# Where the low halves of the next head's q and k are computed in a stick-breaking attention: GpSimd or VectorE

## The chip, the cores and the metric

One NeuronCore of a Trainium2 chip runs the whole program. The metric is the device time of one execution in microseconds (us). The engines are TensorE (PE; its weight loads are shown as PEld), VectorE (DVE), ScalarE (ACT), GpSimd (POOL) and SyncE (SP), which here only issues DMAs.

## The reference

Two transformer blocks over 1024 positions of width 1024, in float32: a first block (dilated attention, latent attention, a mixture of experts), then a second one of two layers. The change lies in the first layer of the second block, in its stick-breaking attention, 8 heads of 64 dimensions. Cut to what matters:

```python
z = einsum('bthd,bshd->bhts', q[:, q0:kend], k[:, :kend]) * d ** -0.5
strict = s_idx < t_idx
log_beta = log_sigmoid(z)
log_one_minus = where(strict, log_sigmoid(-z), 0.0)
suffix = cumsum(log_one_minus, axis=3, reverse=True) - log_one_minus
w = where(strict, exp(log_beta + suffix), 0.0)
out = einsum('bhts,bshd->bthd', w, v[:, :kend])
```

The kernel computes the same as a product: sigmoid(z) times the running product of sigmoid(-z) over the keys to the right.

## The kernel before

`stick_breaking` is one stage of the program, between the retention and the output mix. It has the chip to itself: stages are separated by barriers. Its work is 64 tiles T: 8 heads of 8 tiles i = 0 to 7, where tile i holds 128 queries and n = (i+1)*128 keys. Every engine runs its own instruction list, written as a function `body(l, T)` that `tiles` unrolls 16 tiles at a time (the first 8 tiles and the last stretch stand apart, three rounds of a loop of 16 between); l is T modulo 16. The engines meet only by semaphores.

What each engine does in its step T, in this order:

- PE (lines 2664 to 2705): the scores of tile T into PSUM buffer `sb_s` (two buffers, so it waits until the scan of tile T-2 has ended); then the transposes of w(T-3) into `sb_t` (one buffer: waits until wT(T-4) is copied out); then the product of wT(T-4) with v into `sb_op`.
- ACT (lines 2717 to 2736): two sigmoids of the scores, sigmoid(z) to `be` and sigmoid(-z) in place; then for wide tiles its part of the copy of wT(T-3); at i = 3 the rounding of the next head's q and k (`split_hi`, lines 2713 and 2714).
- DVE (lines 2756 to 2776): its part of the copy of wT(T-3) (line 2763); the scan of tile T, a running product (line 2768), which reads the scores' PSUM buffer and `ones`; the copy of the result of tile T-4 (`sb_ob`, line 2776). The scan waits until w(T-2) has been computed.
- POOL (lines 2781 to 2799): w(T) = be * pr (line 2787), two operands in SBUF.

The scores are computed from q and k each split in a rounded part (type fp32r in the rows) and the rest. ACT rounds the whole (`qs`, `kh`), and somebody must subtract: `qs[64:128]` = q minus its rounded value (64 partitions by 1024), `kl` = k minus its rounded value (128 by 1024). Each of the two counts 4 on `lo_ok`. The buffers are double, one for each of two heads (u = 0, 1), and the split for head h+1 is made while head h runs. PE waits for both at its head's first tile, and SP waits for them before it loads the raw q and k of the head after next. The first head's split is made on DVE ahead of the loop (`split_lo`, lines 2746 and 2747). Those of the other seven heads are made on POOL: the q part behind w of tile i = 3 (line 2793), the k part behind w of tile i = 4 (line 2798), each with a wait for the w before it and one for its own end.

Of the kernel before, what the change touches and what calls it, by code (L numbers as in the profile page):

```python
# [7 lines left out]
F32 = mybir.dt.float32  # L8
F32R = mybir.dt.float32r
U32 = mybir.dt.uint32  # L10
ALU = mybir.AluOpType
# [3 lines left out]
P = 128  # L15
# [903 lines left out]
def tiles(eng, total, peel, lag, body):  # L919


    for T in range(peel):
        body(T % TURN, T)
    with eng.Fori(0, total // TURN - 1) as r:
        for l in range(peel, peel + TURN):
            body(l % TURN, r * TURN + l)
    for T in range(total - TURN + peel, total + lag):
        body(T % TURN, T)


def active(T, k, total):

    return not isinstance(T, int) or 0 <= T - k < total


def reached(eng, sem, n):

    if not isinstance(n, int) or n > 0:
        eng.wait_ge(sem, n)
# [1643 lines left out]
def stick_breaking(nc, ident, heads, qkT_in, v_in_d, C, out):  # L2583
# [4 lines left out]
    T8, DV = NT, 64  # L2588
    total = heads * T8
    widths = [(i + 1) * P for i in range(T8)]  # L2590
    with stage(nc) as st:
        qraw, kraw = (st.sb("sb_" + n, [P, 2, S]) for n in ("qraw", "kraw"))
        qs, kh, kl = (st.sb("sb_" + n, [P, 2, S], F32R) for n in ("qs", "kh", "kl"))
# [23 lines left out]
        def halves(i):  # L2617

            return min(i + 1, BANK // P), i + 1

        with nc.Block() as block:
# [120 lines left out]
            @block.vector  # L2742
            def _(dve):
                def split_lo(u, n_hi):
                    dve.wait_ge(hi_ok, n_hi)
                    dve.tensor_tensor(qs[64:P, u, :], qraw[64:P, u, :], qs[64:P, u, :].bitcast(F32), ALU.subtract).then_inc(lo_ok, 4)
                    dve.tensor_tensor(kl[:, u, :], kraw[:, u, :], kh[:, u, :].bitcast(F32), ALU.subtract).then_inc(lo_ok, 4)

                dve.memset(ones[:, :], 1.0).then_inc(ones_ok, 1)
                dve.memset(pr[:, :, S:S + 1], 1.0).then_inc(ones_ok, 1)  # L2750
                dve.tensor_copy(eye[:, :], ident[:, :]).then_inc(far_ok, 1)
                dve.wait_ge(consts_in, 16)
                dve.tensor_scalar(far[:, :], masks[:, 1, :], NEG, None, ALU.mult).then_inc(far_ok, 1)
                split_lo(0, 8)
                dve.wait_ge(ones_ok, 2)

                def body(l, T):
                    if active(T, 3, total):
                        m = (l - 3) % TURN
                        a, _ = halves(m % T8)  # L2760
                        reached(dve, turned_a, T - 2)
                        reached(dve, pv_done, T - 4)
                        dve.tensor_copy(wT[:, m % 2, 0:a * P], tps[:, 0:a * P]).then_inc(wT_a, 1)
                    if active(T, 0, total):
                        n = widths[l % T8]
                        dve.wait_ge(om_ok, T + 1)
                        reached(dve, w_ok, T - 1)
                        dve.tensor_tensor_scan(pr[:, l % 2, S - n:S][:, ::-1], sps[l % 2][:, 0:n][:, ::-1], ones[:, 0:n], 1.0,  # L2768
                                               ALU.mult, ALU.mult).then_inc(pr_ok, 1)
                    if active(T, 4, total):  # L2770
                        m = (l - 4) % TURN
                        u, i = m // T8, m % T8
                        reached(dve, pv_done, T - 3)
                        if i == 0:
                            dve.wait_ge(stored[u], T - 4 - 8 * u + 16)
                        dve.tensor_copy(o[:, u, i, :], ops[m % 2][:, 0:DV]).then_inc(o_done, 1)
                tiles(dve, total, 8, 4, body)

            @block.gpsimd
            def _(pool):  # L2780
                def body(l, T):
                    if active(T, 0, total):
                        n = widths[l % T8]
                        pool.wait_ge(be_ok, T + 1)
                        pool.wait_ge(pr_ok, T + 1)
                        reached(pool, turned_b, T - 3)
                        pool.tensor_tensor(w[:, l % 4, 0:n], be[:, l % 4, 0:n], pr[:, l % 2, S - n + 1:S + 1],  # L2787
                                           ALU.mult).then_inc(w_ok, 1)
                        u = 1 - l // T8
                        if l % T8 == 3 and active(T + 5, 0, total):  # L2790
                            pool.wait_ge(hi_ok, T + 5 + 4)
                            pool.wait_ge(w_ok, T + 1)
                            pool.tensor_tensor(qs[64:P, u, :], qraw[64:P, u, :], qs[64:P, u, :].bitcast(F32), ALU.subtract).then_inc(lo_ok, 4)
                            pool.wait_ge(lo_ok, T + 9)
                        if l % T8 == 4 and active(T + 4, 0, total):
                            pool.wait_ge(hi_ok, T + 4 + 8)
                            pool.wait_ge(w_ok, T + 1)
                            pool.tensor_tensor(kl[:, u, :], kraw[:, u, :], kh[:, u, :].bitcast(F32), ALU.subtract).then_inc(lo_ok, 4)
                            pool.wait_ge(lo_ok, T + 12)
                tiles(pool, total, 8, 0, body)  # L2800


# [637 lines left out]
```

## Time and profile before

| what | us |
|---|---|
| median of 3 runs | 2599.95 |
| lowest and highest | 2592.92 and 2613.81 |
| the profiled execution, its own time | 2613.81 |
| its span in the profile | 2612.0 |
| first scan of the stage starts, at | 1717.06 |
| last w of the stage starts, at | 1885.75 |

The profiled execution is one of the three. All places in time below are us from the start of its span. A row of the timeline has the start, the length, the engine, the line, the operation, what it writes and reads, and how often; in brackets the idle time of the engine before it and what ended it. Tiles are told apart by their width: the scan of 128x640 is tile i = 4, 128x768 is i = 5, 128x896 is i = 6, 128x1024 is i = 7.

### The profile page before, as it was taken

The page shows a single profiled execution, that of the slowest core. Times are in us where ns is not written, and L with a number is a line of the kernel's source. Part 1 is how long each engine was busy: PE and PEld are TensorE (multiplying, and loading weights), DVE is VectorE, ACT ScalarE, POOL GpSimd, SP SyncE. Part 2 cuts the span into 40 slices and gives each one's busy share as a digit, 9 for nine tenths or more (in the row PEclk, how much of TensorE's full clock was granted, in tenths as well). Part 3 has the DMA queues.
Part 4 walks back from the last instruction along what each step waited for, and adds up shares of the span by engine and source line. Part 5 has one row for each costly group of instructions (what it writes and reads, how often), then busy time and mean ns, then how long its engine had stood idle before and what let it go on. Part 6 is the DMA issues. An engine that isn't in the chain of part 4 may idle for free. (4 is left out here: it accounts for less than half of the span.)

```text
span 2612.0 us, 34392 instructions
## 1 busy us (share of the span) xinstructions
PE 2218.1 (85%) x12244; PEld 1825.9 (70%) x12244; DVE 1290.0 (49%) x2211; ACT 1029.8 (39%) x1828; POOL 584.1 (22%) x672
## 2 busy tenths in 40 slices
PE   7996997999797599999289997968859799956768
PEld 5885887999685466675278885758748687845657
DVE  3333665555543666665451210357755343417843
ACT  3333654555431255554231210046543233327632
POOL 1003101522010122231110001446522000027822
PEclk9997998999898699999699998579989899987879
DMA  4787776321344399995652312243163424141152
GB/s 152 215 239 198 221 219 165 98 64 40 118 146 171 126 359 370 355 342 209 217 206 97 113 49 77 61 87 73 37 219 108 153 95 148 69 135 47 42 184 90
DMA packets 216721, 399.15 MB, mean 153 GB/s; under 512 B 90513, under 2 KB 111377, under 8 KB 203905
## 3 DMA queue, kind: packets, MB, share of 16 engines
q1 hardware_dynamic: 177008, 314.52, 38.0%
q10 hardware_dynamic: 28384, 61.62, 6.2%
q0 software_dynamic: 11184, 21.13, 2.2%
q8 instruction: 87, 1.43, 0.2%
q14 instruction: 58, 0.47, 0.1%
HBM read 300.16 MB, written 114.85 MB: 159 GB/s over the span
## 5 line engine op out<-in xcount | busy, mean ns | idle before, releaser
L78 PE MATMUL pe_acc<-pe_w,hT 128*128 128x512 f32 x960 | 222.3, 393 | 0.0
L78 PEld LDWEIGHTS pe_acc<-pe_w,hT 128*128 128x128 f32 x960 | 181.7, 190 | 37.8
L78 PE MATMUL ex_gu<-hT,ex_xT 128*128 128x512 f32 x792 | 194.2, 401 | 0.8 <-DVE hT L2349 0.8
L2349 DVE TENSOR_TENSOR hT<-ex_raw,hT 128x2048 fp32r<-128x2048 f32 x66 | 150.9, 2288 | 87.1 <-ACT hT L2320 87.1
L78 PE MATMUL pg_acc<-hT,pg_w 128*128 128x512 f32 x768 | 180.0, 396 | 8.9 <-DVE pg_w L257 8.9
L78 PEld LDWEIGHTS pg_acc<-hT,pg_w 128*128 128x128 f32 x768 | 145.5, 190 | 42.4 <-DVE pg_w L257 9.3
L78 PEld LDWEIGHTS ex_gu<-hT,ex_xT 128*128 128x128 f32 x792 | 147.4, 189 | 34.5 <-DVE hT L2349 1.2
L2320 ACT ACTIVATE hT<-ex_raw 128x2048 fp32r<-128x2048 f32 x66 | 126.2, 1913 | 41.4 <-PEq L47 23.9
L296 DVE COPY pe_o<-pe_acc 128x512 f32<-128x512 f32 x28 | 19.3, 690 | 206.7 <-PE pe_acc L78 206.7
L1725 PE MATMUL ab_op<-ab_v,ab_pT 128*128 128x64 f32 x1024 | 121.3, 272 | 0.0
L2278 PE MATMUL ex_dn<-ex_wd,ex_hT 128*128 128x512 f32 x264 | 118.7, 592 | 0.8 <-ACT ex_hT L2314 0.8
L1725 PEld LDWEIGHTS ab_op<-ab_v,ab_pT 128*128 128x128 f32 x1024 | 119.3, 192 | 0.0
L1736 DVE TENSOR_REDUCE ab_mx<-ab_s 128x1 f32<-128x1024 f32 x64 | 78.4, 1224 | 72.3 <-PE ab_s L1703 72.3
L849 PE MATMUL om_acc<-om_w,hT 128*128 128x512 f32 x384 | 95.5, 408 | 18.0 <-DVE om_w L825 16.6
L78 PE MATMUL pa_acc<-hT,pa_w 128*128 128x512 f32 (+1 forms) x432 | 100.1, 392 | 0.7 <-DVE pa_o L290 0.6
L849 PEld LDWEIGHTS om_acc<-om_w,hT 128*128 128x128 f32 x384 | 74.1, 196 | 36.2 <-DVE om_w L825 19.4
L2787 POOL TENSOR_TENSOR sb_w<-sb_be,sb_pr 128x128 f32<-128x128 f32 (+3 forms) x64 | 76.6, 1205 | 97.3 <-DVE sb_pr L2768 75.4
L2768 DVE TENSOR_TENSOR_SCAN sb_pr<-sb_s,sb_ones 128x128 f32<-128x128 f32 (+3 forms) x64 | 86.7, 1354 | 20.0 <-ACT sb_s L2725 17.6
L849 PE MATMUL am_acc<-am_w,hT 128*128 128x512 f32 x384 | 91.6, 398 | 3.4 <-DVE hT L690 3.4
L1515 ACT ACTIVATE aa_p<-aa_sc,aa_nm 128x256 f32<-128x256 f32 x128 | 63.9, 500 | 75.6 <-DVE aa_nm L1482 74.1
L78 PEld LDWEIGHTS pa_acc<-hT,pa_w 128*128 128x128 f32 (+1 forms) x432 | 77.9, 182 | 22.5 <-DVE pa_o L290 3.2
L849 PE MATMUL em_acc<-em_w,hT 128*128 128x512 f32 x384 | 91.2, 397 | 2.6 <-DVE hT L690 2.6
(473 smaller groups left out, 4990.9 us busy)
## 6 DMA issues: line engine op xcount, KB each, us to landing
ex_raw<-in_w_gate SPq DMA_DIRECT2D x33, 1024.0 KB, 7.2
ex_raw<-in_w_up SPq DMA_DIRECT2D x33, 1024.0 KB, 11.1
ex_wd<-in_w_down SPq DMA_DIRECT2D x33, 1024.0 KB, 14.2
pe_raw<-in_even_w_in SPq DMA_DIRECT2D x6, 2048.0 KB, 9.1
pg_raw<-in_odd_w_in SPq DMA_DIRECT2D x5, 2048.0 KB, 9.4
scr_q<-pa_o SPq DMA_DIRECT2D x32, 256.0 KB, 3.8
scr_k<-pa_o SPq DMA_DIRECT2D x32, 256.0 KB, 3.8
hT<-scr_k SPq DMA_DIRECT2D x16, 512.0 KB, 6.8
```

The costliest lines, as they stand in the source:

```text
L78: mm = pe.matmul(out, a(p, k), b(q, k), start=(k == 0 and i == 0), stop=(k == n - 1 and i == 2))
L296: dve.tensor_copy(obuf[0:m, u, 0:n], acc[u][0:m, 0:n]).then_inc(copied[u], 1)
L849: mm = pe.matmul(acc[t % 2][:, nn], hT[:, p, k, t * P:(t + 1) * P], w[:, q, k, nn], start=(i == 0 and j == 0), stop=(i == 7 and j == 2))
L1515: act.activation(p[:, T % 4, a, :], sc[:, T % 2, a, :], ACT.Exp, bias=nm[:, T % 4, a:a + 1], scale=0.125, accum_out=ml[:, a, i, 1, h:h + 1 ...
L1725: mm = pe.matmul(ops[m % 2][:, 0:DV], pT[:, m % 2, k * P:(k + 1) * P], v[:, u, k, :], start=(k == 0), stop=(k == NT - 1))
L1736: dve.reduce_max(mx[:, l:l + 1], sps[l % 2][:, :], AX.X).then_inc(max_done, 1)
L2278: mm = pe.matmul(dn[:, n * BANK:(n + 1) * BANK], hTs[:, b % 2, k, :], wd[:, b % ND, k * D + n * BANK:k * D + (n + 1) * BANK], start=(k == ...
L2320: act.activation(split(s, HI)[:, :, g, :], raw[:, s % NW, g, :].rearrange("p (k n) -> p k n", k=8), ACT.Copy).then_inc(w_hi, 1)
L2349: dve.tensor_tensor(split(s, LO)[:, :, g, :], raw[:, s % NW, g, :].rearrange("p (k n) -> p k n", k=8), split(s, HI)[:, :, g, :].bitcast(F3 ...
L2768: dve.tensor_tensor_scan(pr[:, l % 2, S - n:S][:, ::-1], sps[l % 2][:, 0:n][:, ::-1], ones[:, 0:n], 1.0, ALU.mult, ALU.mult).then_inc(pr_o ...
L2787: pool.tensor_tensor(w[:, l % 4, 0:n], be[:, l % 4, 0:n], pr[:, l % 2, S - n + 1:S + 1], ALU.mult).then_inc(w_ok, 1)
```

## The change

The two subtractions for the next head are taken from POOL and given to DVE, both at i = 4, between the scan of tile 4 and the copy of the result of tile 0, by the function that already does it for the first head. POOL's waits on its own results go too.

```diff
@@ block.vector, body @@
                         dve.tensor_tensor_scan(pr[:, l % 2, S - n:S][:, ::-1], sps[l % 2][:, 0:n][:, ::-1], ones[:, 0:n], 1.0,
                                                ALU.mult, ALU.mult).then_inc(pr_ok, 1)
+                        if l % T8 == 4 and active(T + 4, 0, total):
+                            split_lo(1 - l // T8, T + 4 + 8)
@@ block.gpsimd, body @@
                         pool.tensor_tensor(w[:, l % 4, 0:n], be[:, l % 4, 0:n], pr[:, l % 2, S - n + 1:S + 1],
                                            ALU.mult).then_inc(w_ok, 1)
-                        u = 1 - l // T8
-                        if l % T8 == 3 and active(T + 5, 0, total):
-                            pool.wait_ge(hi_ok, T + 5 + 4)
-                            pool.wait_ge(w_ok, T + 1)
-                            pool.tensor_tensor(qs[64:P, u, :], qraw[64:P, u, :], qs[64:P, u, :].bitcast(F32), ALU.subtract).then_inc(lo_ok, 4)
-                            pool.wait_ge(lo_ok, T + 9)
-                        if l % T8 == 4 and active(T + 4, 0, total):
-                            pool.wait_ge(hi_ok, T + 4 + 8)
-                            pool.wait_ge(w_ok, T + 1)
-                            pool.tensor_tensor(kl[:, u, :], kraw[:, u, :], kh[:, u, :].bitcast(F32), ALU.subtract).then_inc(lo_ok, 4)
-                            pool.wait_ge(lo_ok, T + 12)
```

DVE's list inside the loop, around tile 4 of a head, before (the scan is named SCALAR_TENSOR_TENSOR here; `sb_pr` is its result, `sb_wT` the transposed weights, `sb_ob` the output):

```order
L2763 COPY sb_wT<-sb_t 128x256
L2766 REGISTER_ALU
L2768 SCALAR_TENSOR_TENSOR sb_pr<-sb_s,sb_ones 128x640
L2775 REGISTER_ALU
L2776 COPY sb_ob<-sb_op 128x64
L2763 COPY sb_wT<-sb_t 128x384
L2766 REGISTER_ALU
L2768 SCALAR_TENSOR_TENSOR sb_pr<-sb_s,sb_ones 128x768
```

The same place of DVE's list in the changed kernel:

```order
L2763 COPY sb_wT<-sb_t 128x256
L2766 REGISTER_ALU
L2768 SCALAR_TENSOR_TENSOR sb_pr<-sb_s,sb_ones 128x640
L2745 REGISTER_ALU
L2746 TENSOR_TENSOR sb_qs<-sb_qraw,sb_qs 64x1024
L2747 TENSOR_TENSOR sb_kl<-sb_kraw,sb_kh 128x1024
L2777 REGISTER_ALU
L2778 COPY sb_ob<-sb_op 128x64
L2763 COPY sb_wT<-sb_t 128x384
L2766 REGISTER_ALU
L2768 SCALAR_TENSOR_TENSOR sb_pr<-sb_s,sb_ones 128x768
```

The two subtractions stand ahead of the copy of tile 0's result, of the wT copy of tile 2 (128x384) and of the scan of tile 5.

POOL's list inside the loop, tiles 3 to 6, before:

```order
L2787 TENSOR_TENSOR sb_w<-sb_be,sb_pr 128x512
L2791 REGISTER_ALU
L2793 TENSOR_TENSOR sb_qs<-sb_qraw,sb_qs 64x1024
L2784 REGISTER_ALU
L2787 TENSOR_TENSOR sb_w<-sb_be,sb_pr 128x640
L2796 REGISTER_ALU
L2798 TENSOR_TENSOR sb_kl<-sb_kraw,sb_kh 128x1024
L2784 REGISTER_ALU
L2787 TENSOR_TENSOR sb_w<-sb_be,sb_pr 128x768
```

And in the changed kernel:

```order
L2789 TENSOR_TENSOR sb_w<-sb_be,sb_pr 128x512
L2786 REGISTER_ALU
L2789 TENSOR_TENSOR sb_w<-sb_be,sb_pr 128x640
L2786 REGISTER_ALU
L2789 TENSOR_TENSOR sb_w<-sb_be,sb_pr 128x768
```

POOL has only the w of each tile left. The lists of PE, ACT and SP are the same in both kernels.

## Rows read from the trace of the kernel before

**Rows 1.** Stretches: length, busy PE, PEld, DVE, ACT, POOL (x count), clock, DMA, GB/s.

```profile
1745.00:1766.00 21.00, 18.77 (x140) 16.94 (x140) 16.06 (x25) 13.52 (x23) 14.30 (x10) 1.00 0.35 76
...
257.80:261.20 3.40, 3.40 (x19) 3.40 (x18) 1.72 (x8) 1.67 (x6) 1.40 (x4) 0.50 1.06 382
...
2396.00:2404.80 8.80, 3.26 (x67) 2.79 (x62) 5.97 (x14) 8.71 (x15) 4.29 (x6) 1.00 0.97 241
```

**Rows 2.** Groups of instructions of POOL: a subtraction that moves.

```profile
L2798 POOL TENSOR_TENSOR sb_kl<-sb_kraw,sb_kh 128x1024 fp32r<-128x1024 f32 x7 | 16.6, 2375 | 1.2 <-POOL sb_w L2787 1.2
```

**Rows 3.** Timeline of DVE: scan 4 of the second head, third head's tiles 4 to 7.

```profile
1749.31 1.49 DVE L2768 TENSOR_TENSOR_SCAN sb_pr<-sb_s,sb_ones 128x640 f32<-128x640 f32 x1 [0.79 <-ACT sb_s L2725]
...
1770.44 1.49 DVE L2768 TENSOR_TENSOR_SCAN sb_pr<-sb_s,sb_ones 128x640 f32<-128x640 f32 x1 [0.79 <-ACT sb_s L2725]
...
1771.96 0.55 DVE L2763 COPY sb_wT<-sb_t 128x384 f32<-128x384 f32 x1
1772.78 1.76 DVE L2768 TENSOR_TENSOR_SCAN sb_pr<-sb_s,sb_ones 128x768 f32<-128x768 f32 x1 [0.27 <-ACT sb_s L2725]
...
1775.21 2.02 DVE L2768 TENSOR_TENSOR_SCAN sb_pr<-sb_s,sb_ones 128x896 f32<-128x896 f32 x1
...
1777.26 0.68 DVE L2763 COPY sb_wT<-sb_t 128x512 f32<-128x512 f32 x1
1778.05 2.29 DVE L2768 TENSOR_TENSOR_SCAN sb_pr<-sb_s,sb_ones 128x1024 f32<-128x1024 f32 x1
```

**Rows 4.** Timeline of POOL, the same head: w of tile 4, then of tiles 5 and 6.

```profile
1772.27 1.32 POOL L2787 TENSOR_TENSOR sb_w<-sb_be,sb_pr 128x640 f32<-128x640 f32 x1 [0.25 <-POOL sb_qs L2793]
...
1776.38 3.28 POOL L2787 TENSOR_TENSOR sb_w<-sb_be,sb_pr 128x768 f32<-128x768 f32 x2 [0.24 <-POOL sb_kl L2798]
```

**Rows 5.** Timeline of PE, the same head: end of scores 6, scores 7, transposes 5.

```profile
1773.06 0.23 PE L2676 MATMUL sb_s<-sb_far,sb_eye 128*128 128x128 f32 x1
...
1774.68 0.47 PE L2673 MATMUL sb_s<-sb_kh,sb_qs 128*128 128x512 f32 x1
...
1778.35 0.84 PE L2685 MATMUL sb_t<-ident,sb_w 128*128 128x128 f32 x6 [0.51 <-ACT sb_wT L2732]
```

**Rows 6.** Timeline of ACT, the same head: second sigmoid of tile 7.

```profile
1777.01 1.01 ACT L2725 ACTIVATE sb_s<-sb_s 128x1024 f32<-128x1024 f32 x1
```

**Rows 7.** Timeline of DVE, ahead of the stage's loop: the first head's two subtractions.

```profile
1712.84 1.22 DVE L2746 TENSOR_TENSOR sb_qs<-sb_qraw,sb_qs 64x1024 fp32r<-64x1024 f32 x1 [1.55 <-ACT sb_kh L2714]
1714.10 1.23 DVE L2747 TENSOR_TENSOR sb_kl<-sb_kraw,sb_kh 128x1024 fp32r<-128x1024 f32 x1
```

**Rows 8.** Timeline of POOL and DVE in the retention stage.

```profile
1629.00 1.86 POOL L2470 TENSOR_TENSOR re_t<-re_x,re_cs 128x256 f32<-128x256 f32 x2
1629.03 1.24 DVE L2532 TENSOR_TENSOR re_dec<-re_rot,re_rowdec 128x512 f32<-128x512 f32 x1 [11.49 <-POOL re_rot L2473]
...
1637.14 0.72 POOL L2472 TENSOR_TENSOR re_rot<-re_t 128x256 f32<-128x256 f32 x1
...
1638.58 0.69 DVE L2532 TENSOR_TENSOR re_dec<-re_rot,re_rowdec 128x512 f32<-128x512 f32 x1 [2.22 <-POOL re_rot L2473]
```

**Rows 9.** Timeline of DVE and POOL behind the mixture of experts.

```profile
1323.87 1.28 DVE L614 SCALAR_TENSOR_TENSOR e_y<-e_e,gates,e_x 128x1024 f32<-128x1024 f32 x1 [1.76 <-issue]
1324.02 1.54 POOL L546 TENSOR_TENSOR e_rs<-e_ms,e_half 128x1 f32<-128x1 f32 x1
1325.19 1.28 DVE L617 SCALAR_TENSOR_TENSOR e_y<-e_e,gates,e_y 128x1024 f32<-128x1024 f32 x1
```

**Rows 10.** Timeline of DVE and PE, the first head: scan 4, transposes 3.

```profile
1724.41 1.49 DVE L2768 TENSOR_TENSOR_SCAN sb_pr<-sb_s,sb_ones 128x640 f32<-128x640 f32 x1 [1.02 <-ACT sb_s L2725]
...
1728.93 1.05 PE L2685 MATMUL sb_t<-ident,sb_w 128*128 128x128 f32 x4
```

**Rows 11.** Timeline of PE in two other stages: gaps ahead of a matmul.

```profile
256.38 0.66 PE L1450 MATMUL aa_op<-aa_vn,aa_pT 128*128 128x64 f32 x4 [1.85 <-DVE aa_pT L1489]
...
2398.66 0.33 PE L3129 MATMUL hg_x<-hg_qk 128*64 128x64 f32 x2 [1.84 <-ACT hg_cross L2986]
```

## The prediction

> **What bounds the kernel now.** I read the busy shares by stretch first. In a steady head of the stick-breaking stage (21 us; scan 4 comes again after 1770.44 - 1749.31 = 21.13 [rows 3]) PE is busy 18.77 us, DVE 16.06, POOL 14.30, and the TensorE clock is granted in full [rows 1]. By shares DVE has 5 us a head to spare, and the change moves about 2.5 us of DVE work in. Shares say nothing of where the idle time lies, so the second view is DVE's timeline over one head [rows 3]: at tile i of a head DVE does wT(i-3), scan(i), ob(i-4). From the scan of i=4 (640 columns, starts 1770.44) to that of i=7 (1024 columns, starts 1778.05) it is all but full. Scan 5 starts 1772.78, where the wT copy before it ends 1772.51 and the next would start 0.04 earlier (1772.47): slack 0.31. Scan 6 starts 1775.21, 0.67 after scan 5 ends, which two copies (ob and wT, 0.2 and 0.68 less their overlaps) fill: no slack. Scan 7 starts 1778.05 where DVE was ready at 1777.26 + 0.68 - 0.04 = 1777.90: slack 0.15; that small wait is for POOL, whose w of tile 5 (the first, some 1.5 us, of the pair at 1776.38) ends about 1777.9 [rows 4]. DVE's idle time lies in tiles 0 to 3, where PE has many transposes and products and sets the pace.
>
> So a head is a chain: PE's order from the end of scan 7 to the scores of tile 4, then ACT, then DVE from scan 4 to scan 7. The new work goes into the last link.
>
> **What is removed.** Seven times two POOL subtractions of 2.37 us, 33.2 us in all (16.6 for each line; one of the two stands in [rows 2]). What waits on POOL there is w(4) at 1772.27, 0.34 after scan 4's end (1771.93), and w(5), which costs scan 7 its 0.15. Nothing else is late behind them. The self-waits go with them. SP's loads for head h+2 wait for the same count, are issued some 2 us earlier or at about the same time, and land a head before they are needed: nothing.
>
> **What is added.** The same two subtractions on DVE behind scan 4, 1.22 and 1.23 us [rows 7], with a start lag of 0.04 before each (their rows at 1712.84 and 1714.10 leave 0.04 between them; other DVE neighbours overlap by 0.08). ACT's halves, which they wait for, are done before scan 4 starts. Bare price: 0.04+1.22+0.04+1.23 = 2.53 us behind scan 4. Queued behind it on DVE are ob(0), wT(2) and scan 5; PE's transposes of tile 3 wait for wT(2), PE's scores of tile 7 for scan 5.
>
> The bare price is the lower bound, since scan 4 also releases w(4) on POOL, and the subtractions and w both read two SBUF operands. The nearest rows are of the retention stage [rows 8]: a DVE instruction of that kind takes 0.69 alone, but 1.24 when it starts 0.03 behind a POOL one (1629.00), and the two POOL ones there take 1.86 together where their like take 0.72 each. One stands still while the other runs. In the MoE epilogue a POOL instruction begins behind a DVE one (1323.87 to 1325.15), ends 1325.56, and the next DVE one starts 1325.19 [rows 9]: POOL came in at the gap of 0.04. I apply both: first subtraction 1771.97 to 1773.19, w(4) waits and then runs 1.18 (its 1.32 less the 0.14 start that is behind it), to 1774.37; the second, held meanwhile, runs on for 1.13, to 1775.50. Price 3.57 us. If POOL is not let in at the gap it is 2.53. I take 3.57, because the gap of 0.04 stands in both rows 7 and rows 9.
>
> The page "SBUF — State Buffer" of the Trainium skill, section "SBUF: two separate sides", says that a DVE instruction with two SBUF inputs and a GpSimd instruction that reads SBUF exclude each other for the whole instruction, whoever is first. By that rule the sum is the one with 3.57, without it 2.53; rows 8 agree.
>
> **A steady head.** DVE's path: 3.57 - 0.31 - 0.15 = 3.11 later at scan 7. ACT's path: scan 5 ends 1772.47+3.57+1.76 = 1777.80; PE's scores of tile 7 start 0.06 later. From their start before (1774.68 [rows 5]) to the second sigmoid's end (1778.02 [rows 6]) it is 3.34, and 0.03 more to a scan: 1781.23, which is 3.2 later than 1778.05. So scan 7 is 3.2 us late. Next on PE are the transposes of tile 5 at 1778.35, released by ACT's wT copy behind that sigmoid, then the scores of tile 1 and the transposes of tile 6, released by scan 7 and the DVE copy behind it: all shift alike, and in PE's stretch nothing gives the time back. Six heads (the 2nd to the 7th; the last has no split): 19.2 us. With 2.53 the same working gives 2.17 a head, 13.0.
>
> **The first head** runs at half clock and has room: scan 4 ends 1724.41 + 1.49 = 1725.90, PE's transposes of tile 3 start only at 1728.93 [rows 10]. Subtractions to 1729.47; the wT(2) copy (0.55) to 1730.05, so the transposes start some 1.2 late, and the rest with them: +1.2 (with 2.53: 0.1).
>
> **The clock.** PE now stands between the end of scores 6 (1773.29 [rows 5]) and the end of wT(2): 1775.50 + 0.55 + 0.1 = 1776.15, a gap of 2.86 us where there is none today. After a gap of 1.85 before 256.38 [rows 11] the granted clock fell to 0.5 from 257.8 to 261.2 [rows 1]; after one of 1.84 before 2398.66 it stayed [rows 11, 1]. A low stretch of 3.4 us costs at most half its length, 1.7, and nothing where PE isn't what is waited for. Bounds 0 and 6 x 1.7 = 10.2; I take 4 us in all (a fall in four heads, 1 us each).
>
> **Sum.** 19.2 + 1.2 + 4 = 24 us. The stage has no work beside it and ends in a barrier, so the next stage starts that much later. The profiled execution took 2613.81 (span 2612.0): 2638 by it. It was the slowest of the three; against their median of 2599.95 it is 2624.
>
> **Rivals.**
> A: POOL isn't let in at the gap, or DVE isn't held by it. For it: in its favour only that no row shows a long POOL instruction slipping between two DVE ones; the row at 1325 is a short one. 13.0+0.1, and 1 or 2 for the clock (the gap is 1.8 us): 2614.
> B: POOL was the engine to relieve, and DVE's idle 5 us takes the work in. For it: the shares of rows 1, the wait of scan 7 for w(5). It gives the small waits back, 0.34 x 7 = 2.4: 2597.5, and would be decided if DVE's free time lay behind scan 4. Against: rows 3.
> C, clearly slower: the clock falls in every head, and for two low stretches, since PE after the gap waits again for wT and scan 5 at low duty. Place: from tile 7 into the next head's tiles 0 and 1, which PE sets. 20.4 + 6 x 3.4 = 41, 2641. It decides when low stretches reach past scan 7. Against: within the first head the clock rose while PE had waits too.
>
> **How the numbers follow.** Forecast 0.47, A 0.28, C 0.15, B 0.06, the rest something unseen. About 1% is what a measurement of this kernel can tell from no change; that is 26 us, and the forecast's 24 is just inside it. Its own range, 2612 to 2636, goes over 1% in some 45 of 100; C does throughout, A hardly: slower 0.38. Faster by 1% has no mechanism, 0.03. Same 0.59. The range holds A and the half of C: 2604 to 2643.
>
> **What would show it.** Right: DVE's two subtractions behind each 640-column scan; the second 2.3 us long, not 1.23; w(4) about 2.3 to 2.4 instead of 1.32; the period from one scan 4 to the next 24.2 us or a bit over instead of 21.1; PE's transposes of tile 3 with some 2.8 us of idle before them, released by DVE's wT; low clock of a few us in the stage after 1740. Wrong: a second subtraction of 1.23 (then A), a period of 21 (then B), other stages changed in length.

## The result, and the profile after

The changed kernel takes 2628.48 us (median of 4 runs, 2624.34 to 2632.24) against 2596.43 us for the kernel before (median of 4): the ratio is 1.0115, 95% interval 1.0084 to 1.0147, 30 us by the ratio and 32 by the medians. The forecast was 24 us slower.

The profiled execution of the changed kernel has a span of 2623.3 us, only 11.3 above that of the kernel before. Two stages moved, in opposite ways. The first group of rows is the busy time in stretches (length, then busy us and instruction count of PE, PEld, DVE, ACT and POOL, granted clock, DMA share, GB/s) of the kernel before: the retention stage, then the stick-breaking stage.

```profile
1617.00:1700.00 83.00, 68.45 (x304) 49.70 (x304) 24.25 (x57) 5.14 (x16) 34.77 (x48) 0.55 0.26 80
1717.00:1888.00 171.00, 151.20 (x1065) 135.84 (x1066) 128.24 (x188) 105.83 (x170) 109.77 (x78) 0.94 0.26 58
```

The same two stages in the changed kernel, and then three pieces of the second: from the scan of tile 4 of one head to that of the next, for the second, third and fourth head.

```profile
1622.00:1681.00 59.00, 44.80 (x304) 32.86 (x304) 24.48 (x57) 5.25 (x16) 34.92 (x48) 0.83 0.36 112
1697.50:1900.10 202.60, 167.87 (x1070) 150.86 (x1070) 152.03 (x202) 106.75 (x171) 83.67 (x64) 0.85 0.22 48
1730.98:1759.80 28.82, 24.24 (x141) 22.57 (x140) 19.59 (x26) 13.75 (x22) 10.57 (x8) 0.76 0.25 55
1759.80:1786.01 26.21, 21.40 (x143) 19.13 (x142) 19.57 (x27) 13.75 (x22) 10.58 (x8) 0.87 0.27 61
1786.01:1812.01 26.00, 21.35 (x141) 19.39 (x140) 19.61 (x27) 13.75 (x22) 10.58 (x8) 0.87 0.28 61
```

Stick-breaking went from 170.7 us (first scan to end of the last w) to 202.6, which is 31.9 more, and fits. The retention stage, which the change doesn't touch, took 83 us in the profiled execution before and 59 in the one after: it ran at a granted clock of 0.55 in one and 0.83 in the other. The same unchanged stage took 58 to 64 us in seven of the nine profiled executions here and 83 in two (see the end), so I take this as chance and not as the change. It is why the two spans must not simply be subtracted. A head took 21.09 us on the mean before (scan 4 to scan 4, 2nd to 7th head) and takes 26.21 now.

Inside a head, DVE's timeline of the changed kernel, to be held against [rows 3]:

```profile
1730.98 1.49 DVE L2768 TENSOR_TENSOR_SCAN sb_pr<-sb_s,sb_ones 128x640 f32<-128x640 f32 x1 [0.79 <-ACT sb_s L2725]
...
1759.80 1.49 DVE L2768 TENSOR_TENSOR_SCAN sb_pr<-sb_s,sb_ones 128x640 f32<-128x640 f32 x1 [0.79 <-ACT sb_s L2725]
1761.33 1.22 DVE L2746 TENSOR_TENSOR sb_qs<-sb_qraw,sb_qs 64x1024 fp32r<-64x1024 f32 x1
1762.58 2.23 DVE L2747 TENSOR_TENSOR sb_kl<-sb_kraw,sb_kh 128x1024 fp32r<-128x1024 f32 x1
...
1764.86 0.54 DVE L2763 COPY sb_wT<-sb_t 128x384 f32<-128x384 f32 x1
1765.33 1.74 DVE L2768 TENSOR_TENSOR_SCAN sb_pr<-sb_s,sb_ones 128x768 f32<-128x768 f32 x1
...
1767.70 2.01 DVE L2768 TENSOR_TENSOR_SCAN sb_pr<-sb_s,sb_ones 128x896 f32<-128x896 f32 x1
...
1771.31 0.69 DVE L2763 COPY sb_wT<-sb_t 128x512 f32<-128x512 f32 x1 [1.48 <-PE sb_t L2685]
1772.55 2.29 DVE L2768 TENSOR_TENSOR_SCAN sb_pr<-sb_s,sb_ones 128x1024 f32<-128x1024 f32 x1 [0.55 <-ACT sb_s L2725]
```

The k subtraction takes 2.23 us, where the same instruction takes 1.23 in [rows 7]. From scan 4 to scan 5 it is now 5.53 us; before it was 2.34. And scan 7 no longer follows at once behind scan 6: DVE waits 1.48 us for PE's transposes and 0.55 us for ACT. POOL in the same head:

```profile
1761.43 2.30 POOL L2789 TENSOR_TENSOR sb_w<-sb_be,sb_pr 128x640 f32<-128x640 f32 x1 [2.58 <-DVE sb_pr L2768]
1767.20 1.54 POOL L2789 TENSOR_TENSOR sb_w<-sb_be,sb_pr 128x768 f32<-128x768 f32 x1 [3.48 <-DVE sb_pr L2768]
```

w(4) takes 2.30 us, where [rows 4] has 1.32: it starts 0.10 behind the start of the q subtraction, which ends at 1762.55, and itself ends at 1763.73, 1.18 later; the k subtraction ends at 1764.81, 1.08 after w(4). So each of the two looks as if it had stood while the other ran. PE in the same head, to be held against [rows 5], and ACT's second sigmoid of tile 7 [rows 6]:

```profile
1762.41 0.22 PE L2676 MATMUL sb_s<-sb_far,sb_eye 128*128 128x128 f32 x1
1765.51 1.09 PE L2685 MATMUL sb_t<-ident,sb_w 128*128 128x128 f32 x4 [2.88 <-issue]
1766.98 1.51 PE L2703 MATMUL sb_op<-sb_v,sb_wT 128*128 128x64 f32 x6 [0.39 <-ACTq L2734]
1768.25 0.77 PE L2673 MATMUL sb_s<-sb_kh,sb_qs 128*128 128x512 f32 x1
...
1770.11 0.31 PE L2676 MATMUL sb_s<-sb_far,sb_eye 128*128 128x128 f32 x1
...
1772.85 0.85 PE L2685 MATMUL sb_t<-ident,sb_w 128*128 128x128 f32 x6 [0.17 <-ACT sb_wT L2732]
```

```profile
1771.51 1.01 ACT L2725 ACTIVATE sb_s<-sb_s 128x1024 f32<-128x1024 f32 x1
```

PE stands idle for 2.88 us before the transposes of tile 3, which wait for DVE's copy of wT(2), 1764.86 to 1765.40; in the other five heads from the 2nd to the 7th the gap is 3.02. Behind the gap everything on PE is slow. The clock says why (a stretch of the head before, then two of this one):

```profile
1737.30:1750.90 13.60, 13.30 (x61) 12.94 (x60) 9.24 (x13) 4.38 (x9) 5.93 (x5) 0.50 0.01 1
...
1764.60:1771.40 6.80, 5.50 (x22) 4.78 (x22) 5.32 (x9) 0.95 (x1) 3.10 (x2) 0.50 0.18 39
1771.40:1791.90 20.50, 15.94 (x123) 14.47 (x122) 15.34 (x22) 12.81 (x22) 7.49 (x7) 1.00 0.34 72
```

For 6.8 us from 1764.6 the granted clock is 0.50 (1.2 GHz), then 1.00 again (2.4 GHz); in the head before it stayed low for at least the 13.6 us shown. The scores of tile 7 start at 1768.25, where with scan 5 ending at 1767.07 they could have started at 1767.13, because the four transposes take 1.09 us and the product behind them 1.51, and the scores stand behind both in PE's list.

### The profile page after: what moved, and what is told of

Read it like the earlier page. It is cut to its first block and busy times, and to the rows that moved or that the text cites. A ratio compares the mean times of both kernels' runs of the same rounds, so it can differ in the third digit from the quotient of the medians.

```text
span 2623.3 us, 34380 instructions
## 1 busy us (share of the span) xinstructions
PE 2214.6 (84%) x12244; PEld 1828.5 (70%) x12244; DVE 1314.7 (50%) x2225; ACT 1030.5 (39%) x1828; POOL 554.7 (21%) x658
## 3 DMA queue, kind: packets, MB, share of 16 engines
q8 instruction: 87, 1.43, 0.2%
## 5 line engine op out<-in xcount | busy, mean ns | idle before, releaser
L2789 POOL TENSOR_TENSOR sb_w<-sb_be,sb_pr 128x128 f32<-128x128 f32 (+3 forms) x64 | 83.7, 1312 | 148.1 <-DVE sb_pr L2768 139.7
## 6 DMA issues: line engine op xcount, KB each, us to landing
ex_wd<-in_w_down SPq DMA_DIRECT2D x33, 1024.0 KB, 13.6
```

## The experiments

Periods below are from scan 4 of a head to scan 4 of the next, mean over the 2nd to the 7th head; stage lengths are from the first scan to the end of the last w. All come from the profiled execution of the run. Ratios are against runs of the kernel before on the same chip. Compare runs by the period: the first head's own period lies between 23.00 and 26.15 us over the nine profiles, in part because the low clock with which the stage begins ended 13.4 to 14.0 us after the first scan in three of them and 18.5 to 20.5 us after it in the other six, and the stage length carries this too.

**Matmuls against the gap.** Edit, on PE ahead of the scores:

```diff
                         reached(pe, pr_ok, T - 1)
+                        if i == 6 and not (isinstance(T, int) and T < 8):
+                            for _ in range(10):
+                                pe.matmul(sps[l % 2][:, 0:BANK], qs[:, u, i * P:(i + 1) * P], kh[:, u, 0:BANK], start=True, stop=True)
```

> The changed kernel plus ten matmuls of 128x512 whose result is overwritten, put on PE just ahead of the scores of tile 6 in heads 2 to 8, where PE has nothing to do for 2.9 us a little later. They hold the scores of tile 6 back by 2.2 us, to about 1.5 us before DVE is ready for their scan. Theory (two terms: a longer DVE chain and a low clock after the gap): granted clock 1.00 through heads 2 to 7, period from scan 4 to scan 4 down from 26.2 to 24.2 or 24.3 us, second subtraction still 2.23 us, stage from first scan to last w 191 us instead of 202.6, so about 2617 us. Rival (the clock is a bystander and the chain through DVE and the queues is simply longer than I worked out): period stays at 26 or rises, also at full clock.

Measured: 2610.77 us (10 runs), ratio 1.0063 (1.0035 to 1.0090). Period 24.18, stage 192.7. Stretches of the stage and of one head, then PE and DVE in the next head:

```profile
1699.80:1892.50 192.70, 168.70 (x1133) 149.12 (x1134) 151.11 (x202) 105.77 (x170) 83.77 (x64) 0.94 0.23 51
1733.30:1757.50 24.20, 21.20 (x152) 18.80 (x151) 19.51 (x27) 13.65 (x22) 10.60 (x8) 1.00 0.30 67
```

```profile
1759.01 2.56 PE L2672 MATMUL sb_s<-sb_kh,sb_qs 128*128 128x512 f32 x10
...
1763.17 0.63 PE L2688 MATMUL sb_t<-ident,sb_w 128*128 128x128 f32 x4 [0.74 <-issue]
...
1760.24 2.23 DVE L2750 TENSOR_TENSOR sb_kl<-sb_kraw,sb_kh 128x1024 fp32r<-128x1024 f32 x1
```

More work on PE made the stage 9.9 us shorter than in the changed kernel (the two ratios, 1.0063 and 1.0115, have intervals that just touch). The gap is 0.74 us, the clock stays at 1.00 through the head, the k subtraction is as long as before the edit. So the clock is a term of its own, 26.21 - 24.18 = 2.03 us a head, and not a companion of the longer chain. Its rival (the period stays) falls. Taken head by head (period less 24.18), the changed kernel pays 4.6 us where the low stretch was 13.7 us long, 1.8 to 2.0 where it was 6.8 (three heads), 0.9 to 1.0 where it was 3.4 (two heads).

**w(4) behind both subtractions.** Edit, on POOL:

```diff
                         reached(pool, turned_b, T - 3)
+                        if l % T8 == 4 and active(T + 4, 0, total):
+                            pool.wait_ge(lo_ok, T + 12)
                         pool.tensor_tensor(w[:, l % 4, 0:n], be[:, l % 4, 0:n], pr[:, l % 2, S - n + 1:S + 1],
```

> The changed kernel with one wait more: POOL starts w of tile 4 only when both subtractions on DVE have ended. Theory (DVE and POOL shut each other out, and w(4) comes in between the two subtractions): second subtraction 1.23 instead of 2.23 us, w(4) 1.32 instead of 2.30, DVE's price 2.5 us, PE's gap 1.8 instead of 2.9 us; period 23.3 us where the clock stays up and up to 25 where it falls after the smaller gap; stage 182 to 193 us. Rival (w(4) is needed early and the added wait makes it worse, or the 2.23 us have another cause such as the buffer's own waits): period 26.2 or more, second subtraction still above 2 us.

Measured: 2617.71 us (10 runs), ratio 1.0087 (1.0054 to 1.0121). Stage 187.8. DVE, POOL and PE in one head:

```profile
1770.16 1.22 DVE L2746 TENSOR_TENSOR sb_qs<-sb_qraw,sb_qs 64x1024 fp32r<-64x1024 f32 x1
1771.41 1.23 DVE L2747 TENSOR_TENSOR sb_kl<-sb_kraw,sb_kh 128x1024 fp32r<-128x1024 f32 x1
```

```profile
1772.72 1.33 POOL L2791 TENSOR_TENSOR sb_w<-sb_be,sb_pr 128x640 f32<-128x640 f32 x1 [5.03 <-DVE sb_kl L2747]
...
1773.34 0.63 PE L2685 MATMUL sb_t<-ident,sb_w 128*128 128x128 f32 x4 [2.02 <-issue]
```

A wait that was added, and with it the lock between the two engines is gone: k 1.23, w(4) 1.33, and nobody is late for w(4). The gap is still 2.0 us (1.8 was expected), and the clock still falls, in five of the six heads: periods 23.82, 23.76, 23.68, 25.15 and 23.89, and 23.16 in the one head without a low stretch. By the whole time this run can't be told from the changed kernel (1.0087 against 1.0115, intervals that overlap; its retention stage took 83 us); the shorter stage is what shows the gain.

**Both.** The changed kernel with the two edits above together.

> Both at once: POOL's w(4) behind the subtractions, and the ten matmuls ahead of the scores of tile 6. Theory: nothing is left but the bare price of DVE, 2.53 less the slack of 0.46 and 0.1 for ACT's way: period 23.3 us, granted clock 1.00 after the first head, stage about 184 us. Rival (there is a third term): period clearly above 23.3.

Measured: period 23.21, in every head between 23.18 and 23.24; stage 184.5. One execution took 2610.33 us. The stage:

```profile
1704.30:1888.80 184.50, 164.81 (x1139) 146.34 (x1140) 144.50 (x202) 106.04 (x171) 76.83 (x64) 0.96 0.24 53
```

Nothing is left beside the bare length of DVE's work. With the wait alone, the one head without a low stretch had 23.16 and no extra matmul in it, which agrees: what the matmuls win is the clock. The three terms of a head are now apart: 23.21 - 21.09 = 2.12 bare, 24.18 - 23.21 = 0.97 for the lock, 26.21 - 24.18 = 2.03 for the clock; together 5.12.

**No gap between the two subtractions.** Edit: `qs[64:P, u, :]` and `qraw[64:P, u, :]` of the q subtraction become `qs[:, u, :]` and `qraw[:, u, :]`; the high part of q is lost with it in half of the partitions.

> The changed kernel with the q subtraction on all 128 partitions instead of 64 to 127 (it spoils the high part of q in partitions 0 to 63, so the scores lose it; the count and the length of the instructions stay). Both subtractions then begin on the same partition. Theory (POOL gets in because DVE leaves 0.04 us between two instructions that begin on different partitions): the two follow each other with an overlap of 0.08 us, w(4) waits for both and takes 3.5 us or more, the second subtraction takes 1.23 us; period as in the run with the wait. Rival (POOL comes in between two DVE instructions whether there is a gap or not): second subtraction 2.2 us, w(4) 2.3 us, period 26.

Measured: period 26.1, stage 201.8, 2616.68 us in one execution. DVE, then POOL, in one head:

```profile
1756.45 1.20 DVE L2746 TENSOR_TENSOR sb_qs<-sb_qraw,sb_qs 128x1024 fp32r<-128x1024 f32 x1
1757.56 2.34 DVE L2747 TENSOR_TENSOR sb_kl<-sb_kraw,sb_kh 128x1024 fp32r<-128x1024 f32 x1
```

```profile
1756.66 2.16 POOL L2789 TENSOR_TENSOR sb_w<-sb_be,sb_pr 128x640 f32<-128x640 f32 x1 [2.58 <-DVE sb_pr L2768]
```

The second instruction now begins 0.09 us before the first ends, so the gap is gone, and still w(4) comes in between: it ends at 1758.82 and k takes 2.34. My theory of the gap falls, its rival holds: POOL, waiting, gets its turn between two DVE instructions with or without a pause.

**Only q moves.** The k subtraction stays on POOL, DVE has

```diff
+                        if l % T8 == 4 and active(T + 4, 0, total):
+                            u = 1 - l // T8
+                            dve.wait_ge(hi_ok, T + 4 + 8)
+                            dve.tensor_tensor(qs[64:P, u, :], qraw[64:P, u, :], qs[64:P, u, :].bitcast(F32), ALU.subtract).then_inc(lo_ok, 4)
```

> Half the change: only the q subtraction goes to DVE behind scan 4, the k subtraction stays on POOL behind w(4). Theory (a head pays what DVE's chain from scan 4 to scan 7 is lengthened by, less its slack of 0.46, and the clock only where PE's gap grows long): price 0.04 + 1.22, so 0.8 us a head, PE's gap ahead of the transposes of tile 3 about 0.7 us and the clock at 1.00: period 21.9 us instead of 21.1, stage some 5 us longer than before. w(4) is held back by the q subtraction to about 2.3 us, and POOL's k subtraction starts later, so w(5) ends near 1779.3 in the times of rows 3 and 4, which is 1.2 us later than scan 7 starts: if that wait counts, the period is 22.4. Rival (work on DVE costs its full length, 2.2 us or more a head as soon as it stands behind scan 4): 23 or more.

Measured: period 22.16 in each of the six heads, within 0.02; stage 175.7; 2597.60 us in one execution. The stage, then DVE, POOL and ACT in one head:

```profile
1697.20:1872.90 175.70, 151.00 (x1064) 133.90 (x1065) 136.76 (x195) 105.71 (x170) 99.99 (x71) 0.96 0.26 56
```

```profile
1751.72 1.22 DVE L2773 TENSOR_TENSOR sb_qs<-sb_qraw,sb_qs 64x1024 fp32r<-64x1024 f32 x1
1752.97 0.22 DVE L2780 COPY sb_ob<-sb_op 128x64 f32<-128x64 f32 x1
...
1758.13 0.68 DVE L2763 COPY sb_wT<-sb_t 128x512 f32<-128x512 f32 x1
1758.91 2.29 DVE L2768 TENSOR_TENSOR_SCAN sb_pr<-sb_s,sb_ones 128x1024 f32<-128x1024 f32 x1
```

```profile
1756.90 3.28 POOL L2791 TENSOR_TENSOR sb_w<-sb_be,sb_pr 128x768 f32<-128x768 f32 x2 [0.24 <-POOL sb_kl L2797]
```

```profile
1757.87 1.01 ACT L2725 ACTIVATE sb_s<-sb_s 128x1024 f32<-128x1024 f32 x1
```

1.07 a head, between the two values that I gave (0.8 and 1.3), and by neither's working: w(5) ends near 1758.4, and scan 7 starts at 1758.91, 0.03 behind the end of ACT's sigmoid, so w(5) isn't waited for. From scan 4 to scan 5 it is now 3.49 us, against 2.17 on the mean of the same six heads before (2.34 in the head of [rows 3], which had more slack at scan 5 than the others): 1.32 more, of which the copy behind the subtraction is 0.11, since it starts 0.03 after its end where it otherwise starts 0.08 before the end of what precedes it. From scan 5 to scan 7 it is 0.25 less than before, where five of the six heads had waited for w(5). The rival's price of 2.2 us or more is far off. Half of the change costs a fifth of the whole: PE's gap is 0.9 us and the clock stays at 1.00, and the lock holds only w(4), since no second subtraction stands on DVE.

**The same work on DVE, two tiles earlier.** ACT's rounding goes from tile 3 to tile 1, and on DVE, in place of the call behind scan 4:

```diff
+                        if l % T8 in (2, 3) and active(T + 8 - l % T8, 0, total):
+                            u = 1 - l // T8
+                            dve.wait_ge(hi_ok, T + 16 - l % T8)
+                            if l % T8 == 2:
+                                dve.tensor_tensor(qs[64:P, u, :], qraw[64:P, u, :], qs[64:P, u, :].bitcast(F32), ALU.subtract).then_inc(lo_ok, 4)
+                            else:
+                                dve.tensor_tensor(kl[:, u, :], kraw[:, u, :], kh[:, u, :].bitcast(F32), ALU.subtract).then_inc(lo_ok, 4)
```

> The same work on the same engine as in the changed kernel, at another place: ACT rounds the next head's q and k at tile 1 instead of 3, DVE subtracts q behind scan 2 and k behind scan 3, where it waits for PE today. Theory (place, not engine or amount, makes the cost): no lengthening, the small waits for POOL at scan 7 go as well: period 20.8 to 21.1 us, clock 1.00, stage 168 to 171 us against 170.7, total equal to before within 0.1 per cent or 2 us better. Rival (2.5 us of DVE work more a head, and the lock against w, cost time wherever they stand): period 22 to 24.

Measured: 2593.93 us (12 runs) against 2591.88 (23 runs) of the kernel before, ratio 1.0007 (0.9985 to 1.0029): no difference. Period 20.91, stage 169.1. The stage, then DVE and POOL:

```profile
1701.60:1870.70 169.10, 148.70 (x1064) 133.37 (x1065) 143.50 (x202) 104.81 (x170) 89.06 (x64) 0.95 0.27 58
```

```profile
1752.01 1.20 DVE L2776 TENSOR_TENSOR sb_kl<-sb_kraw,sb_kh 128x1024 fp32r<-128x1024 f32 x1
...
1754.23 1.49 DVE L2768 TENSOR_TENSOR_SCAN sb_pr<-sb_s,sb_ones 128x640 f32<-128x640 f32 x1 [0.56 <-ACT sb_s L2725]
```

```profile
1752.22 1.93 POOL L2794 TENSOR_TENSOR sb_w<-sb_be,sb_pr 128x512 f32<-128x512 f32 x1 [1.12 <-DVE sb_pr L2768]
```

Same engine and same amount, and it costs nothing, since scan 4 waits for ACT anyway. The lock is there too, but it holds only POOL (w(3) takes 1.93 instead of 1.09, k 1.20): the two subtractions no longer follow each other, so none of them stands behind a w. The place, which includes their standing apart, made the 32 us, and neither the engine nor the amount.

**Earlier on POOL.** The kernel before with ACT's rounding at tile 1 and POOL's subtractions behind w(2) and w(3):

```diff
-                        if l % T8 == 3 and active(T + 5, 0, total):
-                            pool.wait_ge(hi_ok, T + 5 + 4)
+                        if l % T8 == 2 and active(T + 6, 0, total):
+                            pool.wait_ge(hi_ok, T + 6 + 8)
...
-                        if l % T8 == 4 and active(T + 4, 0, total):
-                            pool.wait_ge(hi_ok, T + 4 + 8)
+                        if l % T8 == 3 and active(T + 5, 0, total):
+                            pool.wait_ge(hi_ok, T + 5 + 8)
```

> The kernel before with the same earlier places: ACT rounds at tile 1, POOL subtracts q behind w(2) and k behind w(3), where it idles 2 us or more a tile; DVE has none of it. Theory: only the small waits behind POOL go (w(4) and w(5) in time): period 20.7 to 20.9 instead of 21.1, stage 168 to 169 us, 2 us in 2600, at the edge of what can be measured. Rival (POOL was worth relieving for more than that): stage below 166 us. Second rival (PE's transposes now wait for w(2) or w(3), which the subtractions hold back): period above 21.3.

Measured: 2587.07 us (12 runs), ratio 0.9991 (0.9974 to 1.0007), no difference that can be told. Period 20.94, a little over the 20.7 to 20.9 expected; stage 170.7 where 168 to 169 was expected (its first head was 0.9 us longer than before). w(4) now follows POOL's last subtraction, and nobody waits for w(5) at scan 7: that scan starts 0.03 us behind ACT's sigmoid in every head, where in the kernel before it started 0.12 to 0.27 behind it in five of the six:

```profile
1744.81 1.32 POOL L2787 TENSOR_TENSOR sb_w<-sb_be,sb_pr 128x640 f32<-128x640 f32 x1 [0.24 <-POOL sb_kl L2798]
```

0.15 us a head is all that this place of POOL's subtractions had cost. Both early versions beat the changed kernel; neither can be told from the kernel before.

## Why the prediction was right, point by point

- **The place.** DVE is all but full from scan 4 to scan 7, work put there lengthens the head, and what follows gives nothing back. Right: the time from scan 7 to the next scan 4 was 13.46 us before and is 13.45 to 13.49 in the changed kernel, apart from the head with the long low stretch (16.62), and the early version shows that the same work elsewhere is free. One reading in it was wrong: in the head of [rows 3] scan 7 waited its 0.15 us not for POOL's w(5) but for ACT's second sigmoid, which ends at 1778.02 [rows 6], 0.03 ahead of the scan. In the kernel before scans 4, 5 and 6 of every head start 0.02 to 0.04 behind ACT's sigmoid as well, so the way from a scan over PE's scores and ACT to the scan after next was as tight there as DVE's own list. The price did not suffer, since the 3.2 us were taken from ACT's path.
- **The bare price** of 2.53, less the slack: forecast 2.17 a head, measured 2.12.
- **The lock:** forecast 1.04 a head (3.57 against 2.53), measured 0.97; k was to take about 2.3 us and takes 2.23; w(4) 2.3 to 2.4, and takes 2.30. The Trainium skill's rule ("SBUF — State Buffer", section "SBUF: two separate sides") that such a pair shuts each other out for whole instructions gave the same sum. The trace agrees: w(4) ends 1.18 us behind the q subtraction and k 1.08 behind w(4), and with the two ordered by a wait they take 1.33 and 1.23. The reason that I gave for choosing this end of the range, the 0.04 us gap that lets POOL in, was wrong: without the gap it comes in too. Nor do [rows 9] show it, for the DVE instruction at 1325.19 takes 1.28 us like the one before it, so POOL's, though it ends only at 1325.56, did not hold it. That the two instructions shut each other out stood on [rows 8]; that POOL would get its turn was right by luck.
- **The first head:** forecast +1.2, measured 26.13 - 24.90 = 1.23. The closeness proves little: the two profiles happen to agree in when the clock rose (18.7 and 19.3 us after the first scan), and where only q moves this head took 23.47, 1.43 less than before although DVE had more to do, with a clock that rose after 13.4.
- **The period** at full clock: forecast 24.2, measured 24.18 in the run that holds the clock up.
- **The clock** is the term that was mis-sized: forecast 4 us in all, "a fall in four heads, 1 us each", bounded by 10.2. Measured 6 x 2.03 = 12.2, above my upper bound. The gap came out nearly as worked out (2.86 forecast, 2.88 and five times 3.02 measured), and the fall came in six heads of six. The step that failed is the bound, which took each low stretch as 3.4 us long, from the one row at 257.8. In the changed kernel they are twice 3.4, three times 6.8 and once 13.7 us, 6.8 on the mean. What they cost, 0.26 to 0.34 us per us of low clock, was below the half that I allowed.
- **Rivals.** A (POOL not let in) fell by the 2.23. B (POOL was the engine to relieve) fell: the early version with both subtractions off POOL gains 0.18 us a head, and 0.15 of that comes with POOL still doing both. The Trainium skill's "GPSIMD Engine Reference", section "4.1 Engine selection", advises VectorE for elementwise work because GpSimd is about twice as slow on two inputs. The trace agrees on the instruction, 1.23 against 2.37 us, and still the kernel loses 30 us with the work at tile 4 of VectorE's list, and gains nothing that can be told with it two tiles earlier: the slow engine had the time. C (two low stretches in every head, 41 us) named what happened to the clock: 6.8 us of low clock a head on the mean, twice the 3.4. But it priced them at 20.4 us where 12.2 were measured, and only one head of six had a low stretch that reached past scan 7. It was half right.

The whole: 13.0 bare and 6.2 for the lock were forecast for the six heads, 12.7 and 5.8 found; 1.2 and 1.23 for the first; 4 and 12.2 for the clock: 24 against 31.9 in the profile and 32 between the medians. The range of 2604 to 2643 held it. That it went just over 1%, where I had put the forecast just under, is the clock's part.

## What to carry to other kernels

An engine that is idle a quarter of the time can still be full in the one stretch that sets the pace: look for the idle time at the place where the new work would stand, and move the work a few steps to where the engine waits anyway. When something new makes PE wait two or three microseconds in a busy stretch, price the low clock behind it as well as the wait; here it was two fifths of the loss, and ten useless matmuls ahead of the gap won it back. And where a GpSimd and a VectorE instruction that each read two SBUF operands are released by the same event, as here, one of them stands; here a wait that orders them was cheaper than leaving them to meet (0.97 us a head).

## What the runs showed of the hardware

- A waiting GpSimd instruction got its turn between two VectorE instructions, with a pause of 0.03 us between them (the second took 2.23 instead of 1.23 us) and also where the second starts 0.09 us before the first ends (2.34 instead of 1.20).
- After idle gaps on PE of 2.0 us the granted clock fell in five heads of six, after 2.9 to 3.0 us in twelve of twelve (the changed kernel and the one without a gap between the subtractions). It stayed low for 3.4 to 13.7 us; in the longest stretch PE was busy for 13.3 of the 13.6 us shown. After gaps of 0.7 to 0.9 us (ten matmuls; only q moves) it fell in none of twelve heads.
- A us of low clock cost 0.26 to 0.34 us in the changed kernel.
- The retention stage, the same in all kernels here, took 58 to 64 us in seven of the nine profiled executions and 83 us in two (that of the kernel before and that with the wait on POOL). What differs between them is how long the clock stayed low at its start. Single executions of this program can't be compared closer than some 25 us; the stage of the change can.
